# Strassen's seven products for the FFN up projections of a hybrid decoder step, with the gated tiles held in DRAM

## The reference, cut to what matters

```python
def _swiglu(x, w_gate, w_up, w_down):
    return (jax.nn.silu(x @ w_gate) * (x @ w_up)) @ w_down

x = _layernorm(ALPHA * x + 0.5 * _swiglu(x, lp['ffa_w_gate'], lp['ffa_w_up'], lp['ffa_w_down']), ...)
m, ckv, kr, wkv, buf = _token_mixer(x, ...)
x = _layernorm(ALPHA * x + m, ...)
x = _layernorm(ALPHA * x + 0.5 * _swiglu(x, lp['ffb_w_gate'], lp['ffb_w_up'], lp['ffb_w_down']), ...)
```

## Time and profile before

| | us |
|---|---|
| median of 3 runs | 2794.45 (2793.03 to 2797.0) |
| the profiled execution, its own time | 2803.04 |
| its span | 2801.4 |
| PE busy | 2584.0 |
| DVE busy | 1107.6 |
| ACT busy | 845.1 |
| second FFN, from its first load to the end of the span | 838.4 |

### The profile page before, as it was taken

One profiled execution on the slowest core, in us unless ns is written; L12 is line 12 of the kernel. 1 busy time (PEld: TensorE's weight loads), 2 busy tenths in 40 slices (PEclk: granted clock), 3 DMA queues, 4 the chain that ended last, 5 costly groups with the idle time before them and its releaser, 6 DMA issues. The chain is left out here.

```text
span 2801.4 us, 48349 instructions
## 1 busy us (share of the span) xinstructions
PE 2584.0 (92%) x20512; PEld 2191.4 (78%) x20512; DVE 1107.6 (40%) x1870; ACT 845.1 (30%) x1278; POOL 224.1 (8%) x269
## 2 busy tenths in 40 slices
PE   8999999999968998799797999878899999999996
PEld 6888899998756788466545988766688889999875
DVE  3333324322243747466423444433333332432224
ACT  3222223222124746333222333321222222322212
POOL 0000001000021111000000122413000000100002
PEclk9999999999988999899888998989899999999998
DMA  5333333422215443422102111052533333333221
GB/s 165 102 98 111 107 98 94 125 87 82 77 56 164 115 112 98 117 63 61 54 1 111 39 59 50 16 198 84 171 100 96 113 105 98 99 121 87 83 76 56
DMA packets 318180, 262.65 MB, mean 94 GB/s; under 512 B 23026, under 2 KB 277059, under 8 KB 316435
## 3 DMA queue, kind: packets, MB, share of 16 engines
q1 hardware_dynamic: 294450, 243.06, 27.9%
q10 hardware_dynamic: 22304, 13.76, 1.6%
q0 software_dynamic: 1216, 2.80, 0.4%
HBM read 225.51 MB, written 33.53 MB: 92 GB/s over the span
## 5 line engine op out<-in xcount | busy, mean ns | idle before, releaser
L527 DVE TENSOR_TENSOR wlo_a<-wraw_a,whi_a 128x1024 fp32r<-128x1024 f32 x132 | 161.8, 1226 | 361.1 <-ACT whi_a L463 361.1
L527 DVE TENSOR_TENSOR wlo_b<-wraw_b,whi_b 128x1024 fp32r<-128x1024 f32 x132 | 161.8, 1226 | 360.6 <-ACT whi_b L463 360.6
L385 PE MATMUL ps_a<-xhi_a,whi_a 128*128 128x288 f32 (+1 forms) x1056 | 288.9, 328 | 2.4 <-DVE xlo_a L521 2.4
L385 PE MATMUL ps_b<-xhi_b,whi_b 128*128 128x288 f32 (+1 forms) x1056 | 288.7, 328 | 2.4 <-DVE xlo_b L521 2.4
L385 PE MATMUL ps_a<-xlo_a,whi_a 128*128 128x288 f32 (+1 forms) x1056 | 288.7, 328 | 0.0
L385 PE MATMUL ps_b<-xhi_b,wlo_b 128*128 128x288 f32 (+1 forms) x1056 | 288.5, 328 | 0.0
L385 PE MATMUL ps_a<-xhi_a,wlo_a 128*128 128x288 f32 (+1 forms) x1056 | 288.5, 328 | 0.0
L385 PE MATMUL ps_b<-xlo_b,whi_b 128*128 128x288 f32 (+1 forms) x1056 | 288.3, 328 | 0.0
L463 ACT ACTIVATE whi_a<-wraw_a 128x1024 fp32r<-128x1024 f32 x132 | 139.6, 1058 | 387.9 <-PE ps_a L393 210.8
L463 ACT ACTIVATE whi_b<-wraw_b 128x1024 fp32r<-128x1024 f32 x132 | 139.6, 1058 | 387.4 <-PE ps_b L393 210.8
L385 PEld LDWEIGHTS ps_a<-xhi_a,whi_a 128*128 128x128 f32 x1056 | 180.3, 189 | 16.7 <-DVE xlo_a L521 2.8
(11 more groups left out here) (365 smaller groups left out, 4270.2 us busy)
## 6 DMA issues: line engine op xcount, KB each, us to landing
wraw_a<-in_ffa_w_gate SPq DMA_DIRECT2D x44, 512.0 KB, 3.7
wraw_a<-in_ffa_w_up SPq DMA_DIRECT2D x44, 512.0 KB, 3.7
wraw_a<-in_ffa_w_down SPq DMA_DIRECT2D x44, 512.0 KB, 3.3
wraw_b<-in_ffb_w_gate SPq DMA_DIRECT2D x44, 512.0 KB, 3.7
wraw_b<-in_ffb_w_up SPq DMA_DIRECT2D x44, 512.0 KB, 3.7
wraw_b<-in_ffb_w_down SPq DMA_DIRECT2D x44, 512.0 KB, 3.3
wraw_pj<-in_w_in SPq DMA_DIRECT2D x28, 512.0 KB, 3.9
IN_rk<-prep SPq DMA_DIRECT2D x10, 1344.0 KB, 7.0
```

Source lines behind the costliest of these rows:

```text
L385: last = nc.tensor.matmul(ps[:, up_banks(b, f)[g] + p, :c], w[:, s % 2, k * P:(k + 1) * P], x[:, k, o:o + c], start=(k == 0 and n == 0), s ...
L527: V.tensor_tensor(wlo[:, s % 2, :], wraw[:, s % WR, :], whi[:, s % 2, :].bitcast(F32), ALU.subtract).then_inc(Q.w_split.h, 1)
```

## The change

The up projections of all 1088 tokens are made at once. Tokens are halved into 2 x 544 (512 of the prompt and 32 of the sample group each), the model width into 2 x 512 and the 22 column blocks into 2 x 11 (block e with block e + 11). Each product of 2 x 2 quadrants is made by Strassen's seven products in Winograd's form in place of eight. A unit u is one pair of column blocks, gate (even u) or up (odd u), 22 units; a slot i is one of its seven products: 4 k x 3 terms x 2 pieces of 272 columns (`PIECE`), 24 matmuls.

- The seven left operands (four quadrants' sums and three quadrants) are made once at the start, high and low parts, for all tokens (`x_parts`, five items of columns: ACT, DVE and GpSimd share it). They fill `X`; PE starts the first product when all are there. The nine tiles are loaded in `X_ORDER` through four buffers.
- The weights' sums are made by DVE for each unit (`weight_sum`), the splits go into a ring of eight slots of 128 x 512 (`fill`, `WC`), also for the down projection, where a slot is one f.
- Products are added in three pairs of PSUM banks (`bank` in `up_slot`); ACT copies three intermediate states to SBUF (`snapshot`), DVE adds (`add_first`, `combine`). ACT takes silu of the gate quadrants in even units, DVE multiplies in odd ones (in `combine`, and `first_product` for the first quadrant).
- The 22 gated tiles no longer stay in SBUF: after each odd unit ACT sends them to DRAM (`send_hidden`, four DMAs, at slot 1 of the next unit), and SP loads them for the down projection (`load_h`, 44 loads), where they are split (`h_hi`, `h_lo`) over the room of `X`: 14 tiles during the last unit, the others during the down slots.
- The down projection keeps its matmuls (`down_slot`, `last_slots_by_tile(4)`) and changes its PSUM banks. The LayerNorm's instructions stay; `gb` and `bb` come in during the down slots.
- In `ffn` DVE's and GpSimd's internal waits use shared semaphores, the output projection reuses FFN semaphores, and SP clears those of sample attention in `rwkv`, behind its first loads.

```diff
-XS = 5
+XS, WB, WC, HR = 5, 4, 8, 4
 WR = 3
 BLOCKS = ((0, 1, 2, 3), (4, 5, 6, 7, 8))
 PIECES = (((0, 512),), ((0, 288), (288, 288)))
-NC = NF // 2
-UP_STEPS, STEPS = 2 * NF, 2 * NF + 2 * NC
-DOWN_BANKS = (((4, 5, 6, 7), (0, 1, 2, 3)), ((4, 5, 6, 7, 0), (1, 2, 3, 4, 5)))
+HALF, PIECE = 544, 272
+NE, NC = NF // 2, NF // 2
+UNITS = 2 * NE
+UP = 7 * UNITS
+SLOTS = UP + 4 * NF
+F_ORDER = tuple(range(NE - 1)) + tuple(range(NE, NF - 1)) + (NE - 1, NF - 1)
+X_ORDER = (8, 0, 4, 1, 5, 2, 6, 3, 7)
+DOWN_BANKS = (((6, 7, 0, 1), (2, 3, 4, 5)), ((6, 7, 0, 1, 2), (3, 4, 5, 6, 7)))
...
+            def load_h(r):
+                b, f = hidden_load(r)
+                if r >= HR:
+                    sp.wait_ge(Q.hlo_made.h, Q.hlo_made.at(r - HR + 1))
+                sp.wait_ge(Q.h_out.h, Q.h_out.at(64 * (F_ORDER[f] % NE + 1)))
+                src = h_dram[F_ORDER[f]][:, 512 * b:512 + 576 * b]
+                sp.dma_start(hraw[:, r % HR, :512 + 64 * b], src).then_inc(Q.h_in[r % HR].h, 16)
...
+            for k in range(4):
+                load_x(k)
+            for l in range(2):
+                load_w(l)
+            load_x(4)
+            load_x(5)
+            for l in range(2, 4):
+                load_w(l)
+            for k in range(6, 9):
+                load_x(k)
+            for l in range(4, 2 * UNITS):
+                load_w(l)
...
+            def up_slot(u, i):
+                n = 7 * u + i
+                if n == 0:
+                    pe.wait_ge(Q.xlo_made.h, Q.xlo_made.at(15))
+                if n == 1:
+                    pe.wait_ge(Q.slo_made.h, Q.slo_made.at(20))
+                e, g = divmod(u - 1, 2)
...
+                if i == 2:
+                    pe.wait_ge(Q.snap_made.h, Q.snap_made.at(3 * u + 1))
+                if i == 3:
+                    pe.wait_ge(Q.snap_made.h, Q.snap_made.at(3 * u + 2))
+                if i == 4 and u >= 1:
+                    pe.wait_ge(Q.c21_made.h, Q.c21_made.at(u))
+                if i == 5:
+                    pe.wait_ge(Q.snap_made.h, Q.snap_made.at(3 * u + 3))
+                if i == 6:
+                    pe.wait_ge(Q.c22_made.h, Q.c22_made.at(u + 1))
+                pe.wait_ge(Q.w_split.h, Q.w_split.at(n + 1))
+                bank = (0, 2, 0, 2, 4, 2, 4)[i]
+                for k in range(4):
+                    for m, (wp, xp) in enumerate(((0, 0), (0, 1), (1, 0))):
+                        for p in range(2):
+                            last = nc.tensor.matmul(ps[:, bank + p, :PIECE], W[:, n % WC, wp, k * P:(k + 1) * P],
+                                                    operand(i, xp)[:, k, p * PIECE:(p + 1) * PIECE],
+                                                    start=(i in (0, 1, 4) and k == 0 and m == 0), stop=(k == 3 and m == 2),
+                                                    skip_group_check=True)
...
+            def down_slot(b, dh, f):
+                pe.wait_ge(Q.w_split.h, Q.w_split.at(UP + (2 * b + dh) * NF + f + 1))
                 if dh == 0:
+                    pe.wait_ge(Q.hlo_made.h, Q.hlo_made.at(b * NF + f + 1))
...
+            def x_parts(q):
+                a11, a12, a21, a22 = quadrants(q)
+                c = cols_of_item(q)
+                act.wait_ge(Q.x_turned.h, Q.x_turned.at(2 * q + 1))
+                if q >= 2:
+                    act.wait_ge(Q.slo_made.h, Q.slo_made.at(4 * (q - 1)))
+                copy(sums(q, 2), a21).then_inc(Q.xraw_made.h, 1)
+                for j, src in ((6, a22), (0, a11), (2, a12)):
+                    copy(operand(j, 0)[:, :, c], src).then_inc(Q.xhi_made.h, 1)
+                for m, j in enumerate((3, 1, 4, 5)):
+                    act.wait_ge(Q.xs_made.h, Q.xs_made.at(4 * q + m + 1))
+                    copy(operand(j, 0)[:, :, c], sums(q, m)).then_inc(Q.shi_made.h, 1)
...
+            def snapshot(u, j):
+                act.wait_ge(Q.slot_done.h, Q.slot_done.at(7 * u + (1, 2, 4)[j]))
...
+                copy(halves(snap[:, j, :]), bank_pair((0, 1, 1)[j])).then_inc(Q.snap_made.h, 1)
...
+            def silu(e, j):
+                u = 2 * e
+                if j == 0:
+                    act.wait_ge(Q.slot_done.h, Q.slot_done.at(7 * u + 3))
+                    if e >= 1:
+                        act.wait_ge(Q.h_out.h, Q.h_out.at(64 * e))
+                    nc.scalar.activation(halves(SG[:, 0, :]), bank_pair(0), ACT.Silu).then_inc(Q.silu_made.h, 1)
+                else:
+                    made, quad = ((Q.c22_made, 3), (Q.c12_made, 2), (Q.c21_made, 1))[j - 1]
+                    act.wait_ge(made.h, made.at(u + 1))
+                    nc.scalar.activation(SG[:, quad, :], SG[:, quad, :], ACT.Silu).then_inc(Q.silu_made.h, 1)
+            def send_hidden(e):
+                act.wait_ge(Q.h_made.h, Q.h_made.at(4 * e + 4))
+                for g in range(2):
+                    src = SG[:, 2 * g:2 * g + 2, :]
+                    out = h_dram[e + NE * g]
+                    act.dma_start(out[:, :TP].rearrange("p (i c) -> p i c", i=2), src[:, :, :512]).then_inc(Q.h_out.h, 16)
+                    act.dma_start(out[:, TP:].rearrange("p (i c) -> p i c", i=2), src[:, :, 512:]).then_inc(Q.h_out.h, 16)
...
+                    if i in (0, 1, 3):
+                        snapshot(u, (0, 1, 0, 2)[i])
+                    if i == 0 and g == 1:
+                        silu(e, 3)
+                    if i == 1 and g == 0 and e >= 1:
+                        send_hidden(e - 1)
+                    if g == 0 and i == 2:
+                        silu(e, 0)
+                    if g == 0 and i == 5:
+                        silu(e, 1)
+                    if g == 0 and i == 6:
+                        silu(e, 2)
...
+                V.tensor_tensor(sums(q, 0), sums(q, 2), a22, ALU.add).then_inc(made.h, 1)
+                low(6, a22)
...
+            def weight_sum(u, j):
+                if j == 0 and u == 0:
+                    dve.wait_ge(Q.slo_made.h, Q.slo_made.at(16))
+                elif j == 0:
+                    dve.wait_ge(Q.w_split.h, Q.w_split.at(7 * u))
...
+                V.tensor_tensor(T[:, j, :], a, b, ALU.subtract).then_inc(Q.t_made.h, 1)
+            def fill(n):
+                if n >= SLOTS:
                     return
+                u, i = divmod(n, 7)
+                if n < UP and i in (0, 2, 4):
+                    for j in {0: (0, 1), 2: (2,), 4: (3,)}[i]:
+                        weight_sum(u, j)
+                dve.wait_ge(Q.w_hi.h, Q.w_hi.at(n + 1))
+                V.tensor_tensor(W[:, n % WC, 1, :], source(n), W[:, n % WC, 0, :].bitcast(F32), ALU.subtract).then_inc(Q.w_split.h, 1)
+            def add_first(u, j):
+                dve.wait_ge(Q.snap_made.h, Q.snap_made.at(3 * u + j + 1))
+                V.tensor_tensor(snap[:, j, :], snap[:, j, :], snap[:, 0, :], ALU.add).then_inc(chain.h, 1)
+                dve.wait_ge(chain.h, chain.next())
+            def combine(u, j):
+                e, g = divmod(u, 2)
+                made, quad, s, bank, i = ((Q.c22_made, 3, 2, 2, 4), (Q.c12_made, 2, 0, 1, 5), (Q.c21_made, 1, 1, 2, 6))[j]
+                dve.wait_ge(Q.slot_done.h, Q.slot_done.at(7 * u + i + 1))
+                if g == 0 and j == 0 and e >= 1:
+                    dve.wait_ge(Q.h_out.h, Q.h_out.at(64 * e))
+                part = halves(snap[:, s, :])
+                out = halves(SG[:, quad, :]) if g == 0 else part
+                V.tensor_tensor(out, part, bank_pair(bank), ALU.add).then_inc(made.h, 1)
+                if g == 1:
+                    dve.wait_ge(made.h, made.at(u + 1))
+                    dve.wait_ge(Q.silu_made.h, Q.silu_made.at(4 * e + j + 2))
+                    V.tensor_tensor(SG[:, quad, :], SG[:, quad, :], snap[:, s, :], ALU.mult).then_inc(Q.h_made.h, 1)
```

More of the change, by code:

```diff
@@ new lines, in _ @@
+            for s in range(2 * NF):
+                load_w(2 * UNITS + s)
+                while r < min(2 * NF, 4 * s - 4 if s < 8 else max(NF + HR, 2 * s - 4)) and s >= 3:
+                    load_h(r)
+                    r += 1
+                if s == 8:
+                    sp.wait_ge(Q.w_split.h, Q.w_split.at(UP))
+                    sp.dma_start(gb, g_dram.to_broadcast([P, D])).then_inc(Q.gb_in.h, 16)
+                    sp.dma_start(bb, b_dram.to_broadcast([P, D])).then_inc(Q.gb_in.h, 16)
+                if 9 <= s < 9 + XS:
+                    load_res(s - 9)
+                if 33 <= s < 37:
+                    store(s - 33)
+                if 36 <= s < 40:
+                    load_res(s - 36 + XS)
@@ new lines, in _ @@
+            send_hidden(NE - 1)
+            for n in range(UP, SLOTS):
+                k = n - UP
+                if 14 + 2 * k < NF:
+                    h_hi(14 + 2 * k)
+                    h_hi(15 + 2 * k)
+                if NF <= k < 2 * NF:
+                    h_hi(k)
+                if 2 * NF + 1 <= k < 2 * NF + 3:
+                    root(2 * (k - 2 * NF - 1))
+                    root(2 * (k - 2 * NF - 1) + 1)
+                if 2 * NF + 3 <= k < 2 * NF + 7:
```

(32 more changed lines are left out.)

648 lines of the change are left out of this document (327 added, 321 removed).

## The result

| kernel | median us | runs | ratio to before (95%) | profiled execution us | its span us |
|---|---|---|---|---|---|
| before | 2793.74 (2791.69 to 2797.0) | 4 | | 2803.04 | 2801.4 |
| after | 2693.55 (2683.81 to 2699.61) | 4 | 0.9637 [0.961, 0.9664] | 2696.43 | 2694.8 |

The change saves 100.2 us where 79.4 were forecast; the interval of the ratio is 94 to 109 us.

The account below looks back on a forecast made before the run. TensorE's work was taken to bound the FFNs, its waits their ends. Per FFN -53.1 - 6.5 + 19.9 = -39.7 us, two FFNs -79.4, so a median of 2715 us; range 2700 to 2764, forecast 2700 to 2735 at 0.64.

Parts of the forecast that it names:

- The price of one matmul: TensorE's up matmuls: 0.418 ns a column plus a constant 13.3 ns, so 126.7 ns at 272 columns.
- Up projections: Up stage of each FFN: 3696 matmuls of 272 columns, 470.1 us with cold start instead of 523.24, -53.1 us.
- Down projections: Down stage of each FFN: same matmuls, no new waits; turned tiles (4.1 us) and last split wait (2.45) go, -6.5 us.
- The start: Each FFN's first load to first up matmul: 37.0 us instead of 17.1, +19.9 us, bounds +15 to +25.
- Rival 4: At the FFN's start the relay doesn't overlap between items: 55 us instead of 37, 2751 us in all, chance 0.04.
- Inside a unit: The seven slots of a unit: other engines' work and handovers covered, no cost; hidden stores tightest, 26 us kept for the range.
- Rival 1: Up stage: the weight load sets the pace below 288 columns, 133.3 ns a matmul stays, 2764 us, chance 0.07.
- Rivals 2 and 3: Hidden stores delay even units' snapshot: 2735 to 2762 us, chance 0.16; later still, slower than before (2829 us), chance 0.07.
- The contended sums: At the FFN's start, two weight sums of SBUF tensors are stretched beside GpSimd to about 3 us; PSUM-reading items aren't.

Follow-up runs that it names:

- b_o256: Kernel before, with the second 288 column piece of block 1's up steps read from column 256 instead of 288; 2781.32 us, one run.
- w256: Kernel after, with its up matmuls narrowed from 272 to 256 columns except the 132 that open an accumulation; 2650.00 us, one run.
- late: Kernel after, with ScalarE issuing each even unit's four hidden stores only when slot 2 is done, not in slot 1; 2706.22 us.
- start: Kernel after, with the first weight split ahead of the first unit's two weight sums on VectorE; 2689.99 us, ratio 0.9622, then 0.9624 in further rounds.
- both: As `start`, and ScalarE makes the next item's raw copy and first high part before this item's last high part; 2687.25 us, ratio 0.9614.

## Why the prediction was right or wrong

**In kind it was right.** TensorE sets the time inside the units, nothing waits there for a snapshot or a combine, the chain has the form that was described, and the time fell by more than a measurement's uncertainty. **In size it was 20.8 us short** against the median and outside the range. 16.5 us of that lie in the FFNs (95.9 against 79.4). The other 4.3 lie within the interval of 94 to 109 us, where the granted clock of the unchanged stages plays; no run assigns them.

- **The price of one matmul: the step that failed.** "At 272 columns it gives 113.3 + 13.3 = 126.7 ns". The constant of 13.3 ns was read at 512 and 288 columns and taken to belong to every matmul. The matmul takes 125.28 ns, so with the columns at 113.3 ns it is 11.95 here. 3696 x 1.4 = 5.2 us an FFN, 10.4 in all, half of the 20.8. The widths gave 11.4 to 13.6 ns in this kernel and b_o256 moved the constant by 1.7 ns at equal width, so the agreement of the two rows of before (both 13.3) was no proof of a line. The lower bound of the range gave the pace 0.7 ns; the measured one was 1.4 away. A pace that is 1% off is 9 us off after 7392 matmuls. What makes the constant 11.95 at this width and place is open.
- **Up projections.** 464.89 us for a forecast of 470.1, with count, width and cold start as foreseen.
- **Down projections.** 262.49/1152 = 227.9 ns a matmul, within 0.5 ns of before, none of the new waits to be seen; with the turned tiles and the last split -7.2 for -6.5.
- **The start.** +17.3 and +18.1 us for +19.9, 4.3 us in all: the second term that was mis-sized. Item 1 begins 8.7 and 9.5 us after the load (9.3 forecast). The relay was sized at 6.0 us an item and is 5.4 to 5.8: in the first FFN's trace items begin at 11.21, 17.04, 22.56 and 27.99 us. The sum used the mean duration of a DVE operation (0.69 us) where the step from one start to the next is 0.60; the records overlap. Four items, half a microsecond shorter each, are the 2 us. The sums were priced at "about 3 us", and are 3.11. Rival 4 (no overlap, 55 us) fell.
- **Inside a unit.** The margin was put at 1.5 us. It is 2.5 us in 17 of the 20 units and 0.7 to 0.9 us in the other three. The stores took 2.3 us to issue (2.2 taken) and begin 0.6 us earlier in the unit than taken. In the 17 units the silu went on 2.2 us after the last of them, where 2.8 was taken; in the three, 3.9 to 4.1 us. No wait came of it, as forecast, but the choice of the 2.8 us row as the price for every unit was not safe.
- **Rival 1** (weight load bound, 133.3 ns) is refuted by w256 directly. Judging TensorE's headroom by how busy the weight load is, as the Trainium skill does beside the share of peak (Perfetto Trace Analysis, Identifying the Most-Contended Engine), would have warned off the change. The traces disagree: the load is busy without a break at 118.3 ns a matmul as well as at 133.3 ns. The prediction set that rule aside by the 107 ns floor of the earlier trace rows, and that was the right row.
- **Rivals 2 and 3** did not occur, but their mechanism is the one that `late` shows, at its place. That its total of 21.3 us is near the 20 expected is partly luck: 1.0 us a unit was expected, most lost 0.5 and five 0.9 to 3.7.
- **The contended sums.** What the Trainium skill states (GPSIMD Engine Reference, the table row on SBUF interfaces), contention between GpSimd and VectorE instructions with two SBUF inputs, agrees with the traces: sums of two SBUF tensors take 1.48 to 1.76 us beside GpSimd and 0.69 without, and operations with a PSUM input stay at 0.68 in the same stretch.

The version that adds `start` (or `both`) to the change is the best that was run, 0.9614 to 0.9624 of before, though against the plain change only the stretch from item 1 to the first up matmul separates it clearly.

## What to carry to other kernels

Price a stream of matmuls by start-to-start time at the width and layout closest to the one meant, and give the constant a range of its own when it is carried to another width or layout: 1 ns times a few thousand matmuls is the width of a range. Price a chain of back-to-back VectorE operations by the distance of their starts, not by their mean duration. Subtract what an unchanged stage gained or lost between two profiles before a difference of profiles is put down to a change, and read a hidden handover as a margin in microseconds, in its worst unit and not in a typical one: the store was free at one slot, with 0.3 to 0.9 us left in the worst units, and cost 19 us one slot later.

## What the runs showed of the hardware

- The constant per fp32r matmul with its own weight load ran from 11.4 ns (256 columns) to 13.6 (304) in the new kernel and was 13.3 at 512 in the old. At 288 columns it was 11.7, 12.8 or 13.3 ns, depending on kernel and on where the second piece begins; one slow start in four (140 or 135 ns among 130 to 132) is three quarters of the 1.7 ns between the two versions of the old kernel.
- The clock was at 0.50 for 12 to 32 us inside one unchanged stage of some 290 us, and the stage took 287.6 to 298.4 us: as much as a tenth of this change's whole gain. Another unchanged stage took 100 or 110 us, with 4 to 5 or 26 to 30 us at 0.50.
- Four stores from SBUF to DRAM held the silu that waits for them until 2.7 us after the start of the last in 17 of 20 units, and 4.4 to 4.7 us in three, the same three units in five profiles. A silu late by 3.0 us used up its 2.5 us of margin and cost TensorE 0.5 us (`late`).
- Beside contended VectorE sums a GpSimd operation on 512 elements took 1.7 us and not 1.27: the contention costs both sides.
